# Context feed-forward: high and low half side by side as one moving operand of 512 columns

## What is computed

```
CTX_LEN = 256
D_FF = 2816

def macaron_ffn(x, mod3, norm_pre, norm_post, w_gate, w_up, w_down):
    h = modulate(rms_norm(x, norm_pre), mod3[:, 0], mod3[:, 1])
    y = (jax.nn.silu(h @ w_gate) * (h @ w_up)) @ w_down
    return x + MACARON_WEIGHT * mod3[:, 2][:, None, :] * rms_norm(y, norm_post)
...
        x = macaron_ffn(x, mod[:, 0:3], *ffn1)
        ctx = macaron_ffn(ctx, mod_ctx[:, 0:3], *ffn1)
```

## Time and profile before

| | us |
|---|---|
| median of 3 runs | 3478.74 |
| lowest, highest | 3475.89, 3483.37 |
| the profiled execution | 3482.64 |
| its span | 3481.3 |
| TensorE busy | 3387.2 (97%) |
| VectorE busy | 1659.6 (48%) |
| ScalarE busy | 1416.6 (41%) |
| context layer, first matmul to the next stage's first | 398.4 to 596.1 |

### The profile page before, as it was taken

The page is one execution under the profiler, slowest core; times in us unless marked ns, Lnnn a source line. Parts: engine busy times, 40 slices in busy tenths (PEclk is TensorE's granted clock), DMA queues, the critical chain, the costliest instruction groups (busy, mean ns, idle before and its releaser), DMA issues.

```text
span 3481.3 us, 43887 instructions
## 1 busy us (share of the span) xinstructions
PE 3387.2 (97%) x16880; PEld 2718.2 (78%) x16880; DVE 1659.6 (48%) x3080; ACT 1416.6 (41%) x2397; POOL 1197.9 (34%) x538
## 2 busy tenths in 40 slices
PE   7999999988999999999999999999999999999998
PEld 5888899885788886877776788887777776778887
DVE  7978566666510115755552343232865462244142
ACT  3223455655532223354444343343354453344242
POOL 1555200000044443434433434444434333334443
PEclk9999999999999999999999999999999999999999
DMA  7565455221133332222222222323323222223332
GB/s 307 195 219 215 128 187 173 85 89 43 49 97 96 98 95 90 94 65 91 85 91 73 91 85 93 102 91 113 93 73 94 79 74 91 88 79 96 101 96 87
DMA packets 117712, 373.23 MB, mean 107 GB/s; under 512 B 15360, under 2 KB 16256, under 8 KB 117120
## 3 DMA queue, kind: packets, MB, share of 16 engines
q1 hardware_dynamic: 115024, 364.74, 32.4%
q10 hardware_dynamic: 2480, 5.68, 0.5%
HBM read 356.73 MB, written 2.10 MB: 103 GB/s over the span
## 4 chain that ended last, share of the span: by engine, by line
PE 84%; DVE 7%; ACT 3%; issue 2%; DMA 2%; POOL 1%; SPq 1%; ACTq 0%; DVEq 0%; POOLq 0%
PE ps L1489 25%; PE ps L1491 24%; PE ps L1490 24%; DVE b L2411 2%; PE ps L1759 2%; PE ps L1776 1%; PE ps L1741 1%; PE ps L1532 1%; ACT b L1840 1%; PE ps L1736 1%; DMA b<-b 1%; PE ps L1549 1%; PE ps L1800 1%; PE ps L1811 1%; DVE b L2281 1%
## 5 line engine op out<-in xcount | busy, mean ns | idle before, releaser
L2778 POOL TENSOR_TENSOR b<-b,b 128x1024 fp32r<-128x1024 f32 (+1 forms) x494 | 1134.2, 2296 | 2216.9 <-ACT b L1840 2214.0
L1489 PE MATMUL ps<-b,b 128*128 128x512 f32 (+1 forms) x4688 | 1770.3, 378 | 35.7 <-DVE b L2270 6.8
L1491 PE MATMUL ps<-b,b 128*128 128x512 f32 (+1 forms) x4688 | 1734.8, 370 | 0.0
L1490 PE MATMUL ps<-b,b 128*128 128x512 f32 (+1 forms) x4688 | 1733.8, 370 | 0.0
L1489 PEld LDWEIGHTS ps<-b,b 128*128 128x128 f32 x4688 | 884.3, 189 | 227.2 <-issue 56.1
L1491 PEld LDWEIGHTS ps<-b,b 128*128 128x128 f32 x4688 | 884.7, 189 | 153.7
L1490 PEld LDWEIGHTS ps<-b,b 128*128 128x128 f32 x4688 | 885.5, 189 | 148.6 <-issue 5.5
L1840 ACT ACTIVATE b<-b 128x1024 fp32r<-128x1024 f32 (+1 forms) x618 | 603.4, 978 | 314.3 <-PE ps L1491 303.4
L2411 DVE CUSTOM_DVE_ANT_0 b<-b,b,b 128x1024 bf16<-128x1024 f32 x108 | 222.3, 2058 | 20.7 <-DMA b<-in_ada 11.4
L1904 ACT ACTIVATE b<-b 128x512 fp32r<-128x512 f32 (+1 forms) x110 | 64.8, 589 | 383.6 <-DVE b L2325 280.9
L2316 DVE SCALAR_TENSOR_TENSOR b<-ps,b,b 128x511 f32<-128x511 f32 x88 | 66.0, 750 | 248.6 <-ACT b L1894 248.6
(11 more groups left out here) (239 smaller groups left out, 2369.7 us busy)
## 6 DMA issues: line engine op xcount, KB each, us to landing
b<-in_w SPq DMA_DIRECT2D x454, 512.0 KB, 3.4
b<-in_ada SPq DMA_DIRECT2D x86, 512.0 KB, 5.0
b<-in_w SPq DMA_DIRECT2D x80, 384.0 KB, 3.0
b<-in_w SPq DMA_DIRECT2D x80, 320.0 KB, 2.9
b<-b SPq DMA_DIRECT2D x160, 64.0 KB, 2.0
b<-in_const SPq DMA_DIRECT2D x24, 256.0 KB, 3.9
b<-in_x SPq DMA_DIRECT2D x2, 1024.0 KB, 11.3
out<-b SPq DMA_DIRECT2D x8, 256.0 KB, 2.0
```

The costliest lines, as they stand in the source:

```text
L1489: pe.matmul(out, a[0], b[0], start=first, stop=False, **kw)
L1490: pe.matmul(out, a[0], b[1], start=False, stop=False, **kw)
L1491: return pe.matmul(out, a[1], b[0], start=False, stop=last, **kw)
L2778: then(pool.tensor_tensor(wlo[j % NS][:, 0:nk * w], raw[j % NR][:, 0:nk * w], whi[j % NS][:, 0:nk * w].bitcast(F32), ALU.subtract), "lop", j)
```

## The change

For f = 1 the high and the low part stand side by side. HC and LW become the two halves of one tile HCL (as they already lay in memory), and the low part of the hidden product goes to columns 256 to 511 of hh. One matmul with the high weights reads both parts as 512 moving columns and fills the whole bank; a second one of 256 columns with the low weights adds to its first half. Each bank then holds two halves that are summed when it is read: ScalarE copies the right half to a tile, VectorE adds the left half. The gate's SiLU and the up product wait for that sum.

```diff
+    HCL = r.get([128, 2, 8, LC], F32R)
+    HC, LW = HCL[:, 0, :, :], HCL[:, 1, :, :]
...
-                    p = three(b[0:rows, 0:N], (wh[:, q:q + rows], wl[:, q:q + rows]), (hi[:, x, 0:N], lo[:, x, 0:N]),
-                              st["first"], st["last"])
+                    if t.get("f") == 1:
+                        both = hh[:, x, :] if t["name"] == "fd" else HCL[:, :, x, :]
+                        pe.matmul(b[:, :], wh[:, q:q + 128], both, start=st["first"], stop=False)
+                        p = pe.matmul(b[:, 0:N], wl[:, q:q + 128], hi[:, x, 0:N], start=False, stop=st["last"])
...
+                        elif f == 1:
+                            act.activation(q[:, 0:N], b[:, N:2 * N], ACT.Copy).then_inc(up("half", i, 0), 1)
+                            at.wait_ge(*n("both", i, 0))
+                            act.activation(q[:, 0:N], q[:, 0:N], ACT.Silu).then_inc(up("silu", f, i), 1)
...
+                        if f == 1:
+                            at.wait_ge(*(n("hl", f, i - 3) if i >= 3 else n("hl", 0, 21)))
+                            act.activation(q[:, 0:N], b[:, N:2 * N], ACT.Copy).then_inc(up("half", i, 1), 1)
                         at.wait_ge(*n("fm", f, i))
                         act.activation(hh[:, i % 11, 0:N], q[:, 0:N], ACT.Copy).then_inc(up("hh", f, i), 1)
...
+                    if f == 1:
+                        half = 0 if name == "fg" else 1
+                        at.wait_ge(*n("half", i, half))
+                        dve.tensor_tensor(q[:, 0:N], b[:, 0:N], q[:, 0:N], ALU.add).then_inc(up("both", i, half), 1)
...
+                        if f == 1:
+                            at.wait_ge(*n("both", i, 1))
+                            dve.tensor_tensor(q[:, 0:N], q[:, 0:N], g[:, 0:N], ALU.mult).then_inc(up("fm", f, i), 1)
...
+                    elif f == 1:
+                        y = yc[:, i, :]
+                        if t["g"] == 0:
+                            at.wait_ge(*n("y0", f, i))
+                            dve.tensor_tensor(y, y, b[:, 0:N], ALU.add).then_inc(up("y0c", f, i), 1)
+                        else:
+                            at.wait_ge(*n("y0c", f, i))
+                            at.wait_ge(*n(*t["full"]))
+                            own(dve.tensor_tensor(y, y, b[:, N:2 * N], ALU.add))
+                            dve.tensor_tensor(y, y, b[:, 0:N], ALU.add).then_inc(up("y1", f, i), 1)
```

More of the change, by code:

```diff
@@ L358, in soft_steps @@
     return [do("sp", s=key, part=part) for part in range(3)]
-FILL = {12: [8, 16, 32, 64, 96, 128], 8: [0, 4, 48, 192, 256, 384, 512], 3: []}
 def idle(c, n):
-    if c is None or n == 0:
-        return []
-    return [do("idle", c=c, n=n, o=FILL[n].pop(0) if FILL[n] else 0)]
+    return [] if c is None or n == 0 else [do("idle", c=c, n=n)]
 def squares(nid, c=None):
@@ L377, in schedule @@
     stream, at, S = plan(), [0], []
-    FILL.update({12: [8, 16, 32, 64, 96, 128], 8: [0, 4, 48, 192, 256, 384, 512], 3: []})
     def fore():
@@ L683 @@
     "act_ret": ("ra1", "rs2", "rl1", "rl2"), "act_yh": ("nfh", "yh"), "act_mg": ("mgh",),
-    "dve_lo": ("lov",), "dve_tap": ("tapv",), "dve_fm": ("fm",), "dve_hl": ("hl",), "dve_y": ("y1", "into"),
+    "act_half": ("half",), "dve_both": ("both",), "dve_y0": ("y0c",), "dve_lo": ("lov",), "dve_tap": ("tapv",), "dve_fm": ("fm",), "dve_hl": ("hl",), "dve_y": ("y1", "into"),
     "dve_square": ("sqa",), "dve_preq": ("pnq",), "dve_pre": ("pnv",), "dve_addq": ("anq",), "dve_add": ("anv",),
@@ L763, in number @@
                     t["freed"] = ("tapv", t["f"], i, 0)
+                elif t["f"] == 1:
+                    t["freed"] = ("both", i, 0)
+                    mark("half", i, 0)
+                    mark(*t["freed"])
                 else:
@@ L771, in number @@
                     t["freed"] = ("tapv", t["f"], i, 1)
+                elif t["f"] == 1:
+                    t["freed"] = ("both", i, 1)
+                    mark("half", i, 1)
+                    mark(*t["freed"])
                 else:
@@ L780, in number @@
                 else:
-                    t["freed"] = ("y0" if t["g"] == 0 else "y1", t["f"], i)
+                    t["freed"] = (("y0c" if t["f"] == 1 else "y0") if t["g"] == 0 else "y1", t["f"], i)
+                    if t["f"] == 1 and t["g"] == 0:
+                        mark("y0", 1, i)
                 mark(*t["freed"])
@@ L1175, in program @@
     RC = r.top
-    HC, LW = r.get([128, 8, LC], F32R), r.get([128, 8, LC], F32R)
+    HCL = r.get([128, 2, 8, LC], F32R)
+    HC, LW = HCL[:, 0, :, :], HCL[:, 1, :, :]
     yx = r.get([128, 8, L])
@@ L1503, in pe_program @@
                     q = rows * st["q"]
-                    p = three(b[0:rows, 0:N], (wh[:, q:q + rows], wl[:, q:q + rows]), (hi[:, x, 0:N], lo[:, x, 0:N]),
-                              st["first"], st["last"])
+                    if t.get("f") == 1:
[3 more added lines that the diff above has]
+                    else:
+                        p = three(b[0:rows, 0:N], (wh[:, q:q + rows], wl[:, q:q + rows]), (hi[:, x, 0:N], lo[:, x, 0:N]),
+                                  st["first"], st["last"])
                 elif k == "mt":
@@ L1548, in pe_program @@
                 for _ in range(st["n"]):
-                    pe.matmul(b[:, :], w[:, 0:128], w[:, st["o"]:st["o"] + 512], start=True, stop=True)
+                    pe.matmul(b[:, :], w[:, 0:128], w[:, 0:512], start=True, stop=True)
             elif k == "back":
@@ L1873, in act_program @@
                 if name not in ("br", "wo2"):
-                    if name != "fu" or t["conv"] is not None:
+                    if name != "fu" or t["conv"] is not None or t["f"] == 1:
                         if name != "fd" or (t["g"] == 0 and t["conv"] is None):
@@ L1909, in act_program @@
                             at.wait_ge(*n("anq", {1: 0, 2: 2}[f], 7))
-                        act.activation(yc[:, i, :] if f == 1 else yx[:, i, :], b[:, 0:N], ACT.Copy).then_inc(
-                            up("y0", f, i), 1)
+                        act.activation(yc[:, i, :] if f == 1 else yx[:, i, :], b[:, N:2 * N] if f == 1 else b[:, 0:N],
+                                       ACT.Copy).then_inc(up("y0", f, i), 1)
                 elif name in ("xb", "cx"):
@@ L2322, in dve_program @@
                         at.wait_ge(*n("silu", f, i))
-                        if cv is None:
+                        if f == 1:
+                            at.wait_ge(*n("both", i, 1))
+                            dve.tensor_tensor(q[:, 0:N], q[:, 0:N], g[:, 0:N], ALU.mult).then_inc(up("fm", f, i), 1)
+                        elif cv is None:
                             at.wait_ge(*n(*t["full"]))
@@ L2330, in dve_program @@
                         at.wait_ge(*n("hh", f, i))
-                        dve.tensor_tensor(hl[:, i % 11, 0:N], q[:, 0:N], hh[:, i % 11, 0:N].bitcast(F32),
+                        low_half = hh[:, i % 11, N:2 * N] if f == 1 else hl[:, i % 11, 0:N]
+                        dve.tensor_tensor(low_half, q[:, 0:N], hh[:, i % 11, 0:N].bitcast(F32),
                                           ALU.subtract).then_inc(up("hl", f, i), 1)
@@ L2339, in dve_program @@
                         dve.tensor_tensor(X[:, i, :], X[:, i, :], b[:, 0:N], ALU.add).then_inc(up("into", f, t["g"], i), 1)
+                    elif f == 1:
[3 more added lines that the diff above has]
+                            dve.tensor_tensor(y, y, b[:, 0:N], ALU.add).then_inc(up("y0c", f, i), 1)
+                        else:
+                            at.wait_ge(*n("y0c", f, i))
+                            at.wait_ge(*n(*t["full"]))
+                            own(dve.tensor_tensor(y, y, b[:, N:2 * N], ALU.add))
+                            dve.tensor_tensor(y, y, b[:, 0:N], ALU.add).then_inc(up("y1", f, i), 1)
                     elif t["g"] == 1:
-                        y = yc[:, i, :] if f == 1 else yx[:, i, :]
+                        y = yx[:, i, :]
                         at.wait_ge(*n("y0", f, i))
```

## The result

The changed kernel takes 3522.34 us in the median (4 runs, 3520.68 to 3526.45), the kernel before 3481.05 (4 runs, 3475.89 to 3484.84): ratio 1.0122, 95% interval 1.011 to 1.0134, so 41 us slower where 34 were forecast. The profiled execution took 3520.68 us with a span of 3519.3, 38.0 above that of before. Three of the kernels further down had one execution far off the others (4213, 9895 and 4812 us); it is left out of their ratios, and where it was the profiled one (down tiles only) there are no phases.

The account below looks back on a forecast made before the run. The prediction took TensorE to bound the kernel before, and the ScalarE-VectorE exchange the changed gate/up halves: 18.3 - 1.2 + 15.3 + 1.6 = +34.0 us on the median 3478.74 gives 3512.7, range 3498 to 3531.

Parts of the forecast that it names:

- First late lo at 415.7: First gate/up half: VectorE's lo, at 414.43 before, is the first delayed and starts at 415.7.
- Ring of 6.45 us a pair: Gate/up halves: ScalarE and VectorE wait for each other in a closed path, 6.45 us per gate/up pair against TensorE's 5.54.
- A woven add costs 1.39 in full: First gate/up half: each residual add interleaved on VectorE lengthens the path by 1.39 us; seven make 9.7.
- hl at 486.7, down tiles as if begun at 483.2: End of first gate/up half: last hl at 486.7, down tiles effectively start at 483.2 instead of 464.9, +18.3 us.
- At the first down tile lo is 1 us early: First down stretch: lo comes 1 us before it is needed, so the copy and added sum stay covered; stretch -1.2 us.
- First half with its down tiles +17.1 us, second with its own +16.9: Context layer: gate/up +18.3 and down -1.2 us first, then gate/up +15.3 (80.4 against 65.1) and down +1.6.
- TensorE idle about 20 us in each half, granted clock 1.00: Expected trace signs in the gate/up halves: TensorE idle about 20 us in each, its clock staying at 1.00.
- the exchange did not hide: Rival, gate/up halves: sum and SiLU overlap lo, a pair takes under 5.54 us; 3471.5 us, chance 0.05.
- the woven steps did not hide: Rival, gate/up halves: interleaved adds and prenorm steps fall into VectorE's waits, saving 22 us; 3490.7 us, chance 0.06.
- the clock fell: Rival, TensorE: clock drops to half at each of 15 long gaps, +20 us; 3533 us, chance 0.09.
- The operand did not stream as two: Rival, TensorE: the two-part operand runs as two matmuls, costing only the first down stretch's 1.2 us; 3514, within the forecast's 0.77.
- 7.2 us to be gained: TensorE, context layer: 528 k-steps each 0.0136 us shorter save 7.2 us if TensorE stays the bound.

Follow-up runs that it names:

- down tiles only: Kernel before with only the context layer's down tiles in the new form, gate and up tiles in the old one; ratio 1.0003 against before.
- thin adds: Changed kernel with the eight woven residual adds cut from 512 to 64 columns; layer 227.9 us, ratio 1.0108 against the kernel before.
- fillers: Changed kernel with unread 512-column matmuls on TensorE ahead of five waits; layer 235.7 us, ratio 1.0122 against the kernel before.
- sum-only kernel: Changed kernel with the 512-column matmul split into two of 256, sums kept; layer 237.1 us, ratio 1.0106 against the kernel before.
- matmuls only: Changed kernel with the new matmuls but banks read as before, right half dropped; layer 194.0 us, ratio 1.0000 against the kernel before.

## Why the prediction was right, and where it was short

The forecast's own steps, one by one:
- *First late lo at 415.7*: it started at 415.67. The three bank copies and the one sum ahead of it are what moved it.
- *Ring of 6.45 us a pair*: 6.52. Eight of nine distances hold to 0.01; sum to product is 0.53 (454.93 to 455.46) where 0.45 was taken from another pair of dependent VectorE instructions. Over 21 pairs this is some 1.5 us.
- *A woven add costs 1.39 in full*: the thin adds say so, and in the change two lo with an add between them stand 4.91 us apart (rows below), and 3.53 at the same place of the pair without one (453.79 to 457.32).
- *hl at 486.7, down tiles as if begun at 483.2*: TensorE's wait for hl ended at 487.70, so 484.2.
- *At the first down tile lo is 1 us early*: this step failed. Behind hl TensorE waited again, 0.67 us for the next lo (row below): lo stands behind hl in VectorE's queue, so where hl is late, the next lo is. The same came in the second half (0.57 us). By the starts, the k-step took 1.29 us instead of 0.35 both times, 0.9 more each.
- *First half with its down tiles +17.1 us, second with its own +16.9*: measured +19.2 and +19.1. In the first, 1.0 is the late hl and 0.9 the late lo. In the second, hl ended TensorE's wait at 600.35, as if the down tiles had begun at 596.9, where the forecast's 80.4 leads to 596.2, so 0.7; they then took 37.6 us instead of 36.0, of which the late lo has 0.9 and the clock 0.7 (fillers).
- *TensorE idle about 20 us in each half, granted clock 1.00*: neither sign came so. By the starts the halves are 22.9 and 17.7 us longer than 176 k-steps of 0.3464, but only 13.2 and 10.9 us of them are idle in the records. The rest is k-steps of 0.64 us at the lower clock (some 4 us in the first half), and records of matmuls that reach into the waits.
- *Layer +34.0, 232 us*: +38.3, 236.1. All these errors point one way, so no luck with cancelling terms is in the 34.

VectorE's lo around a woven add, changed kernel:

```profile
430.08 1.23 DVE L2298 TENSOR_TENSOR b<-b,b 128x1024 fp32r<-128x1024 f32 x1 [1.43 <-ACT b L1850]
...
434.99 1.23 DVE L2298 TENSOR_TENSOR b<-b,b 128x1024 fp32r<-128x1024 f32 x1 [0.45 <-ACT b L1850]
```

TensorE at the first down tile, changed kernel:

```profile
487.70 0.50 PE L1511 MATMUL ps<-b,b 128*128 128x512 f32 x1 [1.56 <-DVE b L2356]
...
488.99 0.47 PE L1511 MATMUL ps<-b,b 128*128 128x512 f32 x1 [0.67 <-DVE b L2298]
```

Of the 9.6 us between 3512.7 and 3522.34, 2.3 are the median of before, which rose to 3481.05 with its fourth run, 4.3 the layer, and 3 lie between medians and profiled executions (38.0 in the two traces, 41.3 in the medians), with no cause shown.

The rivals: the exchange did not hide, since the sum-only kernel was as slow as the change; the woven steps did not hide; the clock fell, after waits of 1.85 to 2.6 us, at four places (417, 436, 555 and 600 us), not at fifteen, and almost for nothing. The price I set on it left out that a late chunk only shortens the next wait: behind the dip at 417 TensorE has no wait of over 0.6 us before the one that ends at 436.36. The operand did not stream as two. The last point of the forecast on TensorE, 7.2 us to be gained, is right by k-step, but matmuls only brought 3.8 of it in the layer: a faster TensorE reaches the waits for the other engines sooner, and the clock fell behind one of them.

## What to carry to other kernels

Two engines that are busy two thirds and half of the time may still have nothing to spare: follow one item of work through both in-order queues, start to start, and compare the length of the closed path with what the fast engine needs. An instruction that is new in such a path does not cost its length but closes the path; ask what stands *behind* the new wait in its queue. Here the cure was free: the independent copy goes ahead of the instruction that waits, and the same work, with 19.8 us more of VectorE than before, fits into slightly less time. But it cures the loss and no more: none of these kernels is measurably faster than the one before, though the layer is shorter by up to 6.2 us.
